# A two-block transformer kernel, opening changed: first key unit ahead of x's right half, four weight units split by chunks, identity products in the pause, values in banks of their own

## The reference, cut to what matters

```python
h = rmsnorm(x, norm_gain[layer])          # per token, then a gain per feature
proj = h @ w_in_ab[j]                     # (256, 1024) @ (1024, 4104)
qa, ka, va, ga, qb, kb_, vb_, gb, fb = split_cols(proj, AB_SIZES)
qa = rmsnorm(to_heads(qa, MOBA_HEADS), moba_q_gain[j])
ka = rmsnorm(to_heads(ka, MOBA_HEADS), moba_k_gain[j])
```

## Time and profile before

| | us |
|---|---|
| median of 3 runs | 972.51 |
| lowest and highest | 971.35, 973.27 |
| the profiled execution's own time | 971.59 |
| its span | 969.8 |
| PE busy | 951.2 (98%) |
| DVE busy | 644.0 (66%) |
| ACT busy | 544.5 (56%) |
| mean granted clock of PE | 0.996 |

### The profile page before, as it was taken

The page is one execution under the profiler, slowest core; times in us unless marked ns, Lnnn a source line. Parts: engine busy times, 40 slices in busy tenths (PEclk is TensorE's granted clock), DMA queues, the critical chain, the costliest instruction groups (busy, mean ns, idle before and its releaser), DMA issues.

```text
span 969.8 us, 14539 instructions
## 1 busy us (share of the span) xinstructions
PE 951.2 (98%) x5536; PEld 825.5 (85%) x5536; DVE 644.0 (66%) x1259; ACT 544.5 (56%) x1035; POOL 34.4 (4%) x83
## 2 busy tenths in 40 slices
PE   8999999999989999999999999999999999999997
PEld 6778888888778999889888888899998898888885
DVE  5868674777765688477656666567864776655664
ACT  6576674657664666466544444465763665444542
POOL 4001000002010000000000000000000000000000
PEclk9999999999999999999999999999999999999999
DMA  9876424554333464435655657665335355665551
GB/s 293 245 176 126 131 88 133 177 186 156 131 96 89 120 162 157 161 92 185 202 174 193 198 175 239 194 174 174 131 132 179 125 170 179 181 207 176 189 180 44
DMA packets 112145, 158.06 MB, mean 163 GB/s; under 512 B 13814, under 2 KB 48972, under 8 KB 112076
## 3 DMA queue, kind: packets, MB, share of 16 engines
q1 hardware_dynamic: 111640, 156.56, 52.5%
q10 hardware_dynamic: 436, 0.56, 0.2%
HBM read 156.06 MB, written 1.05 MB: 162 GB/s over the span
## 4 chain that ended last, share of the span: by engine, by line
PE 90%; DVE 4%; DMA 3%; ACT 1%; issue 1%; SPq 1%; DVEq 0%; ACTq 0%
PE bank L491 21%; PE bank L493 21%; PE bank L492 21%; PE bank L1177 9%; PE bank L1178 5%; PE bank L645 3%; PE bank L545 2%; PE bank L659 2%; PE bank L671 2%; DMA raw<-in_w_in_ab 2%; DVE w_lo L1915 1%; DMA x<-in_x 1%; PE bank L636 1%; PE bank L618 1%; PE bank L1316 1%
## 5 line engine op out<-in xcount | busy, mean ns | idle before, releaser
L1915 DVE TENSOR_TENSOR w_lo<-raw,w_hi 128x1024 fp32r<-128x1024 f32 (+1 forms) x294 | 335.5, 1185 | 138.9 <-ACT w_hi L1394 138.5
L1394 ACT CAST w_hi<-raw 128x1024 fp32r<-128x1024 f32 (+1 forms) x294 | 283.3, 1021 | 129.2 <-DMA raw<-in_mlp_w_in 68.8
L491 PE MATMUL bank<-w_hi,xT 128*128 128x512 f32 (+1 forms) x368 | 146.5, 398 | 4.2 <-ACT mem L1653 2.8
L493 PE MATMUL bank<-w_hi,xT 128*128 128x512 f32 (+1 forms) x368 | 142.5, 387 | 0.0
L492 PE MATMUL bank<-w_lo,xT 128*128 128x512 f32 (+1 forms) x368 | 142.0, 386 | 0.0
L491 PE MATMUL bank<-w_hi,hT_hi 128*128 128x512 f32 (+1 forms) x348 | 137.0, 394 | 0.3
L1177 PE MATMUL bank<-xT,w_hi 128*128 128x512 f32 x384 | 136.0, 398 | 0.0
L493 PE MATMUL bank<-w_hi,hT_lo 128*128 128x512 f32 (+1 forms) x348 | 134.9, 388 | 0.0
L492 PE MATMUL bank<-w_lo,hT_hi 128*128 128x512 f32 (+1 forms) x348 | 134.8, 387 | 0.0
L1178 PE MATMUL bank<-xT,w_lo 128*128 128x256 f32 x384 | 107.8, 281 | 0.0
L491 PE MATMUL bank<-xT,w_hi 128*128 128x256 f32 x368 | 106.0, 288 | 0.4 <-DVE w_lo L1915 0.3
(11 more groups left out here) (278 smaller groups left out, 1340.9 us busy)
## 6 DMA issues: line engine op xcount, KB each, us to landing
raw<-in_mlp_w_in SPq DMA_DIRECT2D x32, 1024.0 KB, 5.2
raw<-in_mlp_w_out SPq DMA_DIRECT2D x32, 1024.0 KB, 5.1
raw<-in_w_in_ab SPq DMA_DIRECT2D x13, 1024.0 KB, 10.8
raw<-in_w_in_cd SPq DMA_DIRECT2D x13, 1024.0 KB, 5.1
raw<-in_xa_w_kv SPq DMA_DIRECT2D x8, 1024.0 KB, 5.0
raw<-in_sb_w_qkv SPq DMA_DIRECT2D x16, 512.0 KB, 4.6
raw<-in_w_out_ab SPq DMA_DIRECT2D x4, 1024.0 KB, 5.2
raw<-in_w_out_cd SPq DMA_DIRECT2D x4, 1024.0 KB, 5.1
```

Source lines behind the costliest of these rows:

```text
L491: pe.matmul(o, wh, ih, start=start, stop=False, skip_group_check=True)
L493: return pe.matmul(o, wl, ih, start=False, stop=stop, skip_group_check=True)
L1394: nc.scalar.copy(w_hi[:, u % SLOTS, a], raw[:, u % SLOTS, a]).then_inc(hi_ready, 1)
L1915: V.tensor_tensor(w_lo[:, u % SLOTS, a], raw[:, u % SLOTS, a], w_hi[:, u % SLOTS, a].bitcast(F32), ALU.subtract).then_inc(lo_ready, 1)
```

## The change

`PIECED` goes from 3 to 4. x's left half is loaded as two halves by token block, each with its own semaphore, and `turn_left` turns the four chunks of block 0, issues two identity products into bank 3, turns the four chunks of block 1 and issues four more. In the first `front`, the transposes of x's right half come ahead of the last chunk of key unit 1 instead of ahead of the whole unit. `va` and `vc` are written to banks 4 and 5. The four pieces of unit 3 are split by ACT behind the squares of x's right half and by DVE behind the pieces of unit 2, ahead of the scale of the norm. The order of the loads stays; unit 3 is loaded by four instructions instead of one.

```diff
--- before.py
+++ after.py
@@ -35,7 +35,7 @@
 UNIT = 2048
 SLOTS = 5
 AHEAD = 4
-PIECED = 3
+PIECED = 4
 ACT_LOADS = 10
 EPS = 1e-6
 BIG = 1e30
@@ -263,7 +263,7 @@
         read = [sem(f"read{b}") for b in range(8)]
         dve_chain, act_chain, pool_chain = sem("dve_chain"), sem("act_chain"), sem("pool_chain")
         first_gains_in = sem("first_gains_in")
-        x_left_in, x_right_in = sem("x_left_in"), sem("x_right_in")
+        x_left_in, x_right_in = [sem(f"x_left_in{t}") for t in range(T)], sem("x_right_in")
         stage_in, small_in, mem_in, final_in = (sem(n) for n in ("stage_in", "small_in", "mem_in", "final_in"))
         x_ready, squares_ready, var_ready, guess_ready = (sem(n) for n in ("x_ready", "squares_ready", "var_ready", "guess_ready"))
         scale_ready, row_ready, mem_ready = sem("scale_ready"), sem("row_ready"), sem("mem_ready")
@@ -719,9 +719,9 @@
                 if half == 1:
                     end_with_unit(key, u, (x_ready, xcount[name] + 2 * n + 2))
 
-            def warm(n):
+            def warm(n, b=7):
                 for _ in range(n):
-                    pe.matmul(banks[7][:, 0:P], ident[:, :], ident[:, :], start=True, stop=True)
+                    pe.matmul(banks[b][:, 0:P], ident[:, :], ident[:, :], start=True, stop=True)
 
             pe.wait_ge(setup_ready, 1)
             warm(4)
@@ -740,12 +740,12 @@
 
             where = {"qa": 0, "ka": 2, "va": 4, "ga": 2, "qc": 0, "kc": 2, "vc": 4, "qb": 0, "kb": 2, "vb": 2, "gb": 0, "gc": 2, "qd": 0, "gd": 3}
 
-            def tok_unit(name, n):
+            def tok_unit(name, n, before_last=None):
 
                 u = names[name, n]
                 if u >= PIECED:
                     take(u, 0)
-                bank_of = lambda t: (where[name] + t) % 4
+                bank_of = lambda t: where[name] + t if where[name] == 4 else (where[name] + t) % 4
                 wh, wl = (flat(w, u).rearrange("p (c n) -> p c n", n=PANEL) for w in (w_hi, w_lo))
                 by_chunk = u < PIECED
                 for one in range(T * 4):
@@ -753,6 +753,8 @@
                     if n == 0 and c == 0:
                         begin((name, t), bank_of(t))
                     k = 4 * n + c
+                    if before_last and one == T * 3:
+                        before_last()
                     if t == 0:
                         if by_chunk:
                             pe.wait_ge(lo_ready, 4 * u + c + 1)
@@ -770,8 +772,11 @@
             def front(name, q, k, v, g):
 
                 tok_unit(q, 0)
-                turn_x(name, 1, 4)
-                tok_unit(k, 0)
+                if q == "qa":
+                    tok_unit(k, 0, lambda: turn_x(name, 1, 4))
+                else:
+                    turn_x(name, 1, 4)
+                    tok_unit(k, 0)
                 tok_unit(q, 1)
                 tok_unit(k, 1)
                 if q == "qa":
@@ -787,14 +792,15 @@
 
             def turn_left():
 
-                warm(2)
-                pe.wait_ge(x_left_in, 16)
                 for c in range(4):
-                    b = 4 + c
-                    begin(((("n", 0), 0), c), b)
-                    for t in range(T):
-                        ins = pe.transpose(banks[b][:, t * P:(t + 1) * P], x[:, t, c * P:(c + 1) * P], ident[:, :])
-                    end(((("n", 0), 0), c), ins, (loT_ready, state["loT"] + c + 1))
+                    begin(((("n", 0), 0), c), 4 + c)
+                for t in range(T):
+                    pe.wait_ge(x_left_in[t], 16)
+                    for c in range(4):
+                        ins = pe.transpose(banks[4 + c][:, t * P:(t + 1) * P], x[:, t, c * P:(c + 1) * P], ident[:, :])
+                        if t == T - 1:
+                            end(((("n", 0), 0), c), ins, (loT_ready, state["loT"] + c + 1))
+                    warm(2 + 2 * t, 3)
                 norms[("n", 0), 0] = chunks_ready(state["loT"])
                 state["loT"] += 4
 
@@ -1461,12 +1467,14 @@
                 for c in range(4):
                     split_piece(1, c)
                 for t in range(T):
-                    x_squares(first, 0, t, (x_left_in, 16))
+                    x_squares(first, 0, t, (x_left_in[t], 16))
                 for c in range(4):
                     hi_one((first, 1), c, xT_hi, 4)
                     split_piece(2, c)
                 for t in range(T):
                     x_squares(first, 1, t, (x_right_in, 16))
+                for c in range(4):
+                    split_piece(3, c)
                 rsqrt(stat[first], T)
                 done[0] = PIECED
                 used(names["qa", 0])
@@ -2674,11 +2684,13 @@
                     sp.dma_start(raw[:, u % SLOTS, c * cols:(c + 1) * cols], ap[:, c, :]).then_inc(piece_in[4 * u + c], 16)
 
             gain_rows(*gain_loads[0])
-            sp.dma_start(x[:, :, 0:PANEL], tok(A["x"])[:, :, 0:PANEL]).then_inc(x_left_in, 16)
+            for t in range(T):
+                sp.dma_start(x[:, t, 0:PANEL], tok(A["x"])[:, t, 0:PANEL]).then_inc(x_left_in[t], 16)
             pieces(0)
             pieces(1)
             sp.dma_start(x[:, :, PANEL:], tok(A["x"])[:, :, PANEL:]).then_inc(x_right_in, 16)
             pieces(2)
+            pieces(3)
             for u in range(PIECED, SLOTS):
                 weight(u)
             for load in gain_loads[ACT_LOADS:]:
```

## The result

The changed kernel took 974.43 us (median of 20 runs, 971.19 to 977.93), the kernel before 972.66 beside it: ratio 1.0017, 95% interval 1.0009 to 1.0025. Forecast were 972.2 us and a range of 970.5 to 973.9. So it is slower by 0.17%, where a gain of 0.03% was expected.

What follows compares the result with a forecast made beforehand. PE was taken to be fed almost everywhere, its wait at line 618 ended by unit 7's landing behind a queue backlog. Earlier arrival would become wait; the landing's 0.3 us made 972.51 - 0.3 = 972.2 us, range 970.5 to 973.9.

Steps and rivals of the forecast that it cites:

- The opening: PE's start up to line 618: second query unit at 21.5 against 21.89, 0.4 us gained of the 1.86 us stop.
- copy chain: Copies and splits after the transposes of x's right half, 3.46 us, forecast as the next wait, before the second query unit.
- rival C: ACT and DVE come too late at the second value unit or unit 8's split: up to 1.0 us, 973.2; chance 0.06.
- The landing of unit 7: Load of the second gate unit, which ends PE's wait at line 618: taken to land 0.3 us earlier, near zero.
- rival B: Clock falls in a longer wait at line 618, of 1.5 to 2.1 us: 1.7 us lost, 974.2; chance 0.07.
- 1.1 us or more: PE's wait at line 618 ahead of the key transposes, forecast to grow to this from 1.07 us.
- chances were counted up to 974.4: Chance 0.06 was given to times above 974.4, 0.11 to times below 970.6, and 0.83 to those within.
- the value banks and the splits: Values in banks 4 and 5: cost nothing, gain nothing; ACT's and DVE's splits: q and k slip some 1.5 us.
- -0.3: Forecast change of the whole time, from line 618's release moving from 46.54 to 46.2: 972.51 to 972.2 us.

Runs made afterwards that it cites:

- repeated comparison: The changed kernel run once more, unaltered, beside the kernel before: 973.94 us against 973.38, ratio 1.0006 (0.9995 to 1.0018).
- pairs with that wait removed: Changed kernel and kernel before, both with queries copied ahead of unit 7's cast (972.58, 972.49 us), or both with forget columns loaded behind unit 7 (971.97, 972.06).
- changed kernel with late columns: Changed kernel with the forget columns' load behind unit 7: 971.97 us; with twelve idle DVE instructions more, which moved the stops, 971.64.
- old kernel with late columns: Kernel before with the forget columns' load moved behind unit 7 in the queue: 972.06 us, ratio 0.9987 (0.9978 to 0.9997).

## Why the prediction was wrong

- **The opening was right.** First product 8.27 (forecast 8.5), second query unit 21.37 (21.5), arrival at line 618 at 44.95 (45.1). The stop moved to the copy chain, 1.03 us, as read.
- **ACT and DVE (rival C): right to count it small.** Unit 4's cast came at 27.48 (27.9), unit 6's splits ended a microsecond sooner than summed, and the first value unit started at 32.91 (33.0).
- **The landing of unit 7 is a step that failed:** "I take 0.3 us earlier". It does not follow the issue, and the pieces do not shorten it. In the six profiles of kernels with the changed order that still wait for it, the cast starts at 43.8 to 45.6, and at 45.1 in that of the kernel before with unit 3 in pieces; in the four with neither it starts at 43.7 to 44.7. The means are 44.8 and 44.0, and from issue to landing pass 16.8 to 18.2 us in the seven and 15.3 to 16.3 in the four. Each is one execution: a landing some tenths later is likely, its size and its cause stay open. The term should have stood at 0 or on the side of a loss, with a scatter of a microsecond, and the whole 0.5 us of earlier arrival been booked as wait.
- **The clock (rival B) had too small a chance for a single execution.** The mechanism and price were right. I set the wait at "1.1 us or more" from one landing; with 0.5 us of lead and a scatter of a microsecond it was 3.16, 1.71, 3.06 and 2.21 us in the four profiles of the changed order in which nothing was done about it. Waits of 2.09, 2.21, 3.06 and 3.16 us were followed by half clock, those of 1.07, 1.44 and 1.71 and the stop of 1.86 were not. The old stop for x can bring half clock too (2.49 us, above), but up to 1.07 us of what it loses could be taken out of the wait at line 618; this is argued, no run shows it. The range did not fit the rivals either: B's own 974.2 lies above its end of 973.9, while the chances were counted up to 974.4.
- **A term was missing:** two more DVE instructions, 0.3 us at 266 and 0.3 at 446 us. I costed the value banks and the splits at nothing beyond 60 us, since no row there concerned them. By its price in the profiles this alone turns -0.3 into +0.3.
- **The sum with what was measured:** 0 or some tenths for the landing, +0.6 for DVE's two stops, and half clock at line 618 in some executions. The repeated comparison gives +0.56 us (973.94 - 973.38), the first +1.77 (974.43 - 972.66). Of the 1.2 between them 0.7 is the unchanged kernel's own median, 972.66 and 973.38.
- **How much of it is the clock.** The estimate (1 - mean clock) x span gives 5.3 us for the changed kernel in the repeated comparison and 5.2 for the kernel before beside it. Of the 0.7 us between their means (973.97 and 973.24) the clock is 0.1, and 0.6 is left. In the first comparison it is 5.6 us for the changed kernel, and 0.9 us of loss are left without the clock, as worked out on record ahead of the repeat. So half clock made the profiled execution slow, while most of the loss in the medians, 0.6 to 0.9 us, is none of the clock's. DVE's stops cover 0.6 to 0.8 of that in the profiles, a later landing would cover a rest; how the two share it stays open.
- **What the opening is worth by itself:** 0.5 us of arrival, once nothing waits at line 618. The pairs with that wait removed come out level, -0.1 and +0.1 us, as they would if DVE's 0.6 us took it back. With the stops moved, the changed kernel with late columns is 1.4 us faster than the kernel before (971.64, ratio 0.9982), of which the late columns alone gave the old kernel 1.3 (973.38 - 972.06). That it also beats the old kernel with late columns by the opening's 0.5 is likely, but the intervals overlap.

## What to carry to other kernels

Follow a saved stall to the next wait and ask what ends that one: if it is a landing with a queue ahead of it, book the saving as a longer wait, with the landing's scatter, and price the clock that may fall in it. A stretch at half clock in one profile says little about the median: the granted clocks of all runs say what share it has. Small loads of many rows that nobody needs soon belong behind the load that PE waits for. And a change of the number of instructions on an engine can move short stops by hundreds of microseconds; a few idle instructions tell such a difference from one of the work.

## What the runs showed of the hardware

- **The clock.** A pause of 2.09 us was followed by 1.2 GHz, one of 1.86 was not. The Trainium skill (TensorE: Matmul & The Clock Gate, section "Why this matters for your kernels") warns of idle gaps between bursts of matmuls, but of longer ones than 2.09, 2.21 and 2.49 us; the measurement decides.
- **Half clock without a pause.** Behind the products of 9 rows of line 825 (819 before) half clock began, between 105.9 and 110.3 us, in eight of the fifteen profiles, PE busy all the while (110.00 to 113.00 above). In four of them no half clock had come earlier. Its cause is open.
- **The queue.** Unit 7's cast started at 45.60 with unit 3 whole and at 43.82 and 45.39 with it in pieces of 256 KB: no sign here that pieces slow a full queue, and too few executions to rule out some tenths. 1,024 rows of 32 bytes ahead of unit 7 did: they landed 7.4 us behind unit 6, and unit 7 another 3.5 us behind them, in the kernel before.
